# Later weight splits inside a chunk, split small projections and earlier top-k rounds in a two-layer transformer kernel on one core

## The reference

```python
h = rms_norm(x, g_norm1) * (1.0 + sc1) + sh1          # sc1, sh1 from silu(c) @ w_mod
proj = h @ w_in                                        # 17 chunks of 256 columns and three small ones
(a_u, a_v, g_q, g_k, g_v, g_r, g_a, d_q, d_k, d_v, d_iq, d_ik, d_iw, gates) = jnp.split(proj, splits, axis=-1)
y_a = gmlp_branch(gelu(a_u), gelu(a_v), ...)
log_alpha = log_sigmoid(g_a @ gla_w_gate2 + gla_b_gate) / 16          # g_a has 16 columns
y_b = rms_norm(gla_scan(g_q, g_k, g_v, log_alpha)) * silu(g_r)
score = sum over 4 heads of relu(d_iq . d_ik) * d_iw                  # d_ik has 64 columns, d_iw 4
y_c = attention of d_q over the 128 keys of the highest score, with d_q, d_k normed per head
mix = (sum of sigmoid(gates) * up projections of y_a, y_b, y_c) @ w_out
x = x + gt1 * mix; x = x + gt2 * hier_moe(norm(x))                    # 16 experts
# second layer: swiglu, then q, k, v, c_b, c_c, c_in = split(norm(h) @ w_in_2)
# forgetting attention over q, k, v; short_conv(c_c * c_in) * c_b; gates, w_out; swiglu
```

## Time and profile before

| | |
|---|---|
| median of 3 runs | 2298.84 us (2297.03 to 2301.77) |
| profiled execution | 2300.81 us |
| its span, first to last instruction | 2299.1 us |
| granted PE clock, mean | 0.945 |
| busy: PE, DVE, ACT, POOL | 94%, 43%, 31%, 27% |
| L662 (w_lo), 133 times | 618.7 us of POOL, 4653 ns each |
| L1501 (w_hi), 133 times | 254.8 us of ACT, 1916 ns each |

### The profile page before, as it was taken

The page is one execution under the profiler, slowest core; times in us unless marked ns, Lnnn a source line. Parts: engine busy times, 40 slices in busy tenths (PEclk is TensorE's granted clock), DMA queues, the critical chain, the costliest instruction groups (busy, mean ns, idle before and its releaser), DMA issues.

```text
span 2299.1 us, 28612 instructions
## 1 busy us (share of the span) xinstructions
PE 2153.3 (94%) x11806; PEld 1789.4 (78%) x11806; DVE 997.4 (43%) x1501; ACT 708.7 (31%) x880; POOL 621.3 (27%) x150
## 2 busy tenths in 40 slices
PE   7899989999998999979999998899899979999997
...
GB/s 242 31 74 56 74 74 39 174 173 195 98 55 160 341 331 332 335 56 76 90 91 91 91 91 56 55 56 48 45 92 92 89 40 92 92 91 92 100 100 37
DMA packets 176218, 261.30 MB, mean 114 GB/s; under 512 B 13209, under 2 KB 141898, under 8 KB 176126
## 3 DMA queue, kind: packets, MB, share of 16 engines
...
## 4 chain that ended last, share of the span: by engine, by line
PE 86%; DVE 7%; DMA 3%; ACT 2%; issue 1%; SPq 0%; ACTq 0%; DVEq 0%
PE PS L700 65%; PE PS L1228 6%; PE PS L1250 4%; DMA w_raw<-in_w_in 2%; DVE Hf L2072 1%; DMA m_raw<-in_w_exp_up 1%; DVE Hf L2053 1%; PE PS L856 1%; PE PS L760 1%; PE PS L1270 1%; PE PS L1194 1%; PE PS L1382 1%; ACT w_hi L1501 1%; DVE R L2084 1%; PE PS L806 1%
## 5 line engine op out<-in xcount | busy, mean ns | idle before, releaser
L662 POOL TENSOR_TENSOR w_lo<-w_raw,w_hi 128x2048 fp32r<-128x2048 f32 x133 | 618.7, 4653 | 1603.6 <-ACT w_hi L1501 1603.6
L700 PE MATMUL PS<-HH,w_hi 128*128 128x512 f32 (+1 forms) x1936 | 603.5, 350 | 43.4 <-DVE HL L2046 27.3
L700 PE MATMUL PS<-HL,w_hi 128*128 128x512 f32 (+1 forms) x1936 | 601.4, 348 | 0.0
L700 PE MATMUL PS<-HH,w_lo 128*128 128x512 f32 (+1 forms) x1936 | 598.3, 347 | 0.0
L1501 ACT ACTIVATE w_hi<-w_raw 128x2048 fp32r<-128x2048 f32 x133 | 254.8, 1916 | 821.1 <-DMA w_raw<-in_w_ffn_in 299.8
L700 PEld LDWEIGHTS PS<-HH,w_hi 128*128 128x128 f32 x1936 | 341.0, 192 | 96.2 <-issue 31.9
L700 PEld LDWEIGHTS PS<-HH,w_lo 128*128 128x128 f32 x1936 | 340.2, 192 | 45.7
L700 PEld LDWEIGHTS PS<-HL,w_hi 128*128 128x128 f32 x1936 | 340.1, 191 | 44.6
L2758 DVE TENSOR_TENSOR actf<-PS,sg 128x528 f32<-128x528 f32 (+1 forms) x44 | 30.8, 700 | 432.7 <-PE PS L700 432.7
L2769 DVE TENSOR_TENSOR yacc<-yacc,PS 128x528 f32<-128x528 f32 (+1 forms) x176 | 122.3, 695 | 106.0 <-PE PS L700 106.0
L2651 DVE TENSOR_TENSOR m_lo<-m_raw,m_hi 128x2048 fp32r<-128x2048 f32 x56 | 128.2, 2292 | 80.1 <-ACT m_hi L1814 79.4
...
## 6 DMA issues: line engine op xcount, KB each, us to landing
...
```

The source lines that it names most:

```text
L662: pool.tensor_tensor(w_lo[:, s, :], w_raw[:, s, :], w_hi[:, s, :].bitcast(F32), ALU.subtract).then_inc(split, 1)
L700: ins = mm(o, l, r, **k)
```

## The change

The small projections become one more tile of 100 columns (d_ik 64, g_a 16, 16 zero columns, d_iw 4): their weights are split by ACT and POOL into w_small_hi and w_small_lo, and PE makes their 24 L700 products between those of the first iq tile. ACT evacuates ga, ik twice, and iw_rows; PE transposes iw_rows. One small load goes.

`next_hi()` moves from ahead of a chunk's first evacuation to its middle, in the chunks gq to u and in K, Q, V, CC, CI, CB of the second layer. With gq, gk the order on ACT becomes: gq tile, relus, w_hi, gate chain, gq tile, relus. DVE does `scores(0)` before the gate's scans and `scores(4)` before `exp_arg`. Five `top_rounds` leave dsa(0) to dsa(3) (2, 2, 2, 2 become 0, 1, 1, 1) and go to the tiles of dv with the head norms (1, 1, 1, 1 become 2, 3, 2, 2).

```diff
@@ -226,3 +226,5 @@
 
-        w_small = ar("w_small", 0, [KT, 148])
+        w_small = ar("w_small", 0, [KT, 100])
+        w_small_lo = ar("w_small_lo", 0, [KT, 100], F32R)
+        w_small_hi = ar("w_small_hi", 3200, [KT, 100], F32R)
         oh_sb = ar("oh_sb", 40960, [640])
...
@@ -528,6 +533,5 @@
             w1 = wk("w_in")
-            sp.dma_start(w_small[:, :, 0:16], w1[:, :, G_A:G_A + 16]).then_inc(small_in, 16)
-            sp.dma_start(w_small[:, :, 16:80], w1[:, :, D_IK:D_IK + 64]).then_inc(small_in, 16)
-            sp.dma_start(w_small[:, :, 80:144], w1[:, :, D_IK:D_IK + 64]).then_inc(small_in, 16)
-            sp.dma_start(w_small[:, :, 144:148], w1[:, :, D_IW:D_IW + 4]).then_inc(small_in, 16)
+            sp.dma_start(w_small[:, :, 0:64], w1[:, :, D_IK:D_IK + 64]).then_inc(small_in, 16)
+            sp.dma_start(w_small[:, :, 64:80], w1[:, :, G_A:G_A + 16]).then_inc(small_in, 16)
+            sp.dma_start(w_small[:, :, 96:100], w1[:, :, D_IW:D_IW + 4]).then_inc(small_in, 16)
             sp.dma_start(w_gate2[0:16, :], a["gla_w_gate2"][0]).then_inc(small_in, 16)
@@ -648,3 +652,4 @@
             pool.memset(sel_sum[:, :], 0.0).then_inc(consts, 1)
-            pool.wait_ge(consts, 7)
+            pool.memset(w_small[:, :, 80:96], 0.0).then_inc(consts, 1)
+            pool.wait_ge(consts, 8)
             pool.memset(sel_sum[:, 3:4], 1.0).then_inc(consts, 1)
@@ -663,2 +668,4 @@
 
+            pool.wait_ge(small_hi, 1)
+            pool.tensor_tensor(w_small_lo[:, :, :], w_small[:, :, :], w_small_hi[:, :, :].bitcast(F32), ALU.subtract).then_inc(small_split, 1)
             for c in range(RING):
@@ -845,20 +852,2 @@
 
-            pe.wait_ge(small_in, 16 * 11)
-            g0, slots = W.g, []
-            ga_group, ik_group = g0, g0 + 1
-            for x in range(3):
-                slots.append(W.claim())
-                W.g += 1
-            W.g = g0
-            for k in range(KT):
-                pe.wait_ge(hh_ready, k + 1)
-                for s, c0, n in ((slots[0], 0, 16), (slots[1], 16, 128)):
-                    ins = mm(PS[0:n, s, 0, :], w_small[:, k, c0:c0 + n], Hf[:, k, 0:SEQ], start=k == 0, stop=k == KT - 1)
-                    if k == KT - 1:
-                        W.made(ins)
-                for t in range(NTOK):
-                    ins = mm(PS[:, slots[2], 0, 4 * t:4 * t + 4], Hf[:, k, P * t:P * t + P], w_small[:, k, 144:148],
-                             start=k == 0 and t == 0, stop=k == KT - 1, skip_group_check=True)
-            W.made(ins)
-            await_h(now=False)
             rh, rlo = h_operands(0, SEQ)
@@ -986,5 +975,25 @@
 
-            fm()
-            iq_group = W.g - 1
-            W.wait_released(ga_group)
+            pe.wait_ge(small_split, 1)
+            s_w = begin_chunk()
+            hi = w_hi[:, s_w, :].rearrange("p (k n) -> p k n", k=KT)
+            lo = w_lo[:, s_w, :].rearrange("p (k n) -> p k n", k=KT)
+            s_iq = W.claim()
+            W.g += 1
+            small_group = W.g
+            s_small = W.claim()
+            W.g -= 1
+            for k in range(KT):
+                pe.wait_ge(hl_ready, hcount["hl"] + k + 1)
+                iq_ins = three(outs_of(s_iq, SEQ), (hi[:, k, 0:P], lo[:, k, 0:P]), (rh(k), rlo(k)), k == 0, k == KT - 1)
+                small_ins = three([(PS[0:100, s_small, 0, :], slice(0, SEQ))], (w_small_hi[:, k, :], w_small_lo[:, k, :]),
+                                  (rh(k), rlo(k)), k == 0, k == KT - 1)
+            hcount["hl"] += KT
+            W.made(iq_ins)
+            W.made(small_ins)
+            s = W.claim()
+            for k in range(KT):
+                ins = three(outs_of(s, SEQ), (hi[:, k, P:2 * P], lo[:, k, P:2 * P]), (rh(k), rlo(k)), k == 0, k == KT - 1)
+            iq_group = W.g
+            W.made(ins)
+            W.wait_released(small_group)
             for j in range(2):
@@ -992,2 +1001,6 @@
                 W.made(mm(PS[:, s, 0, :], w_gate2[0:16, P * j:P * j + P], ga[0:16, 0:SEQ], start=True, stop=True))
+            s = W.claim()
+            for t in range(NTOK):
+                ins = nc.tensor.transpose(PS[:, s, 0, 4 * t:4 * t + 4], iw_rows[0:4, P * t:P * t + P], ident[0:4, 0:4])
+            W.made(ins)
 
...
@@ -1519,2 +1531,5 @@
                 af(squares1[:, k, :], real(k), ACT.Square).then_inc(sq_ready, 1)
+            act.wait_ge(small_in, 16 * 10)
+            act.wait_ge(consts, CONSTS)
+            af(w_small_hi[:, :, :], w_small[:, :, :], ACT.Copy).then_inc(small_hi, 1)
             root(SEQ)
@@ -1524,5 +1539,2 @@
             next_hi()
-            evac(ga[0:16, 0:SEQ], src=lambda s: PS[0:16, s, 0, :])
-            evac(ik[:, :])
-            evac(iw[:, :, :], src=lambda s: PS[:, s, 0, 0:16].rearrange("p (t h) -> p t h", h=4))
 
@@ -1586,2 +1598,7 @@
             evac(iq[:, 0, :])
+            s = W.arrive()
+            af(ga[0:16, 0:SEQ], PS[64:80, s, 0, :], ACT.Copy)
+            af(ik[0:64, :], PS[0:64, s, 0, :], ACT.Copy)
+            af(ik[64:128, :], PS[0:64, s, 0, :], ACT.Copy)
+            W.release(af(iw_rows[0:4, :], PS[96:100, s, 0, :], ACT.Copy))
             evac(iq[:, 1, :])
@@ -1589,4 +1606,9 @@
                 evac(Bc[:, j, :], ACT.Identity, bias=C1[:, V1["gla_b_gate"] + j:V1["gla_b_gate"] + j + 1])
-            W.wait_released(W.g - 2)
-            W.wait_released(W.g - 1)
+            gate_evac = W.g
+            evac(iw[:, :, :], src=lambda s: PS[:, s, 0, 0:16].rearrange("p (t h) -> p t h", h=4))
+            evac(gq[:, 0, :])
+            relus(0)
+            next_hi()
+            W.wait_released(gate_evac - 2)
+            W.wait_released(gate_evac - 1)
             for j in range(2):
@@ -1599,9 +1621,2 @@
                 af((t0, t1)[j][:, :], (t0, t1)[j][:, :], ACT.Ln, bias=eps[:, 1:2]).then_inc(gla_act, 1)
-            next_hi()
-            evac(gq[:, 0, :])
-            act.wait_ge(exp_arg, 1)
-            af(ebl[:, :, :], ebl[:, :, :], ACT.Exp, scale=1.0 / 16).then_inc(gla_act, 1)
-            relus(0)
             evac(gq[:, 1, :])
@@ -1610,9 +1625,10 @@
 
-            next_hi()
             evac(gk[:, 0, :])
             relus(8)
+            next_hi()
             evac(gk[:, 1, :])
+            act.wait_ge(exp_arg, 1)
+            af(ebl[:, :, :], ebl[:, :, :], ACT.Exp, scale=1.0 / 16).then_inc(gla_act, 1)
 
 
-            next_hi()
             for t in range(NTOK):
@@ -1620,3 +1636,4 @@
                 gla_exp(0, t)
-            next_hi()
+                if t == 1:
+                    next_hi()
             for t in range(NTOK):
@@ -1654,2 +1672,4 @@
                 gla_out(2 * t + 1)
+                if t == 0:
+                    next_hi()
 
@@ -1977,4 +1999,5 @@
             for x, c0 in enumerate(KQV):
-                next_hi()
                 for t in range(2 if x % 3 < 2 else 5):
+                    if t == (1 if x % 3 < 2 else 2):
+                        next_hi()
                     s = W.arrive()
@@ -1997,3 +2020,3 @@
             for m in range(12):
-                if m % 2 == 0:
+                if m % 2 == 1:
                     next_hi()
...
@@ -2309,4 +2331,3 @@
 
-            W.skip(4)
-            W.wait_made(W.g - 5)
+            W.skip(6)
             L.mark(v_.memset(Kp[:, :, :], 0.0))
@@ -2315,2 +2336,4 @@
             L(v_.memset(chunks(t2[:, :])[:, :, 0:1], 0.0))
+            W.skip(1)
+            scores(0)
             for j in range(2):
@@ -2322,10 +2345,7 @@
                 L.mark(v_.tensor_copy(ebl[:, j, :], chunks(Bc[:, j, :])[:, :, CHUNK - 1:CHUNK].rearrange("p c t -> p (c t)")))
+            gq_group = W.g
+            W.skip(1)
+            scores(4)
             L.wait()
             dve.sem_inc(exp_arg, 1)
-            for x in (0, 4):
-                W.skip(1)
-                scores(x)
-            gq_group = W.g - 5
             W.skip(1)
@@ -2386,3 +2406,3 @@
             W.skip(1)
-            top_rounds(1)
+            top_rounds(2)
             W.skip(1)
@@ -2392,9 +2412,9 @@
             W.skip(1)
-            top_rounds(1)
+            top_rounds(3)
             W.skip(2)
             head_columns(0)
-            top_rounds(1)
+            top_rounds(2)
             W.skip(1)
             head_columns(1)
-            top_rounds(1)
+            top_rounds(2)
 
@@ -2421,3 +2441,4 @@
                 dsa(n)
-                top_rounds(2)
+                if n > 0:
+                    top_rounds(1)
             for n in range(4, 12):
```

22 lines of the change are left out of this document (12 added, 10 removed).

## The result

| | before | after |
|---|---|---|
| median, 4 runs each | 2297.94 us (2296.87 to 2301.77) | 2265.90 us (2262.68 to 2266.08) |
| profiled execution / its span | 2300.81 / 2299.1 us | 2266.08 / 2264.3 us |

The ratio is 0.9854 [0.9837, 0.9871], 32.0 us faster. The forecast of 2266 and its range were right.

What follows compares the result with a forecast made beforehand. PE's own work was taken as 86% of the chain, so only fewer PE operations, shorter PE waits or less low-clock work help. Gains less the front's loss sum to 32.6 us: 2300.81 to 2268.2, less 2.0 gives 2266 us, range 2256 to 2284.

Steps and rivals of the forecast that it cites:

- A: Small projections, gq and gk: fp32 products replaced and PE's waits for gq and relu_s shortened; gain 8.8 us.
- front: Kernel start: POOL's making of w_small_lo may hold DVE's mod sums and move the first norm; loss of 1.5 us.
- H: Second layer: moving w_hi and POOL's split removes waits for pr and low clock, one collision kept; gain 12.0 us.
- top-k rounds: Five rounds moved from dsa(0..3) to the head norms at dv: 0 us, ends -1 and +1.
- rival 2: GLA factors: a split holds one, eats the 2.8 us cover, and PE waits 1.6 at L893; 2270 us, chance 0.05.
- B: dk chunk: w_hi no longer precedes the evacuations of dk, a wait of 1.0 us.
- C: Inverse roots: w_hi no longer precedes the evacuation of inv_rows, a wait of 1.1 us.
- D, E: First layer's v chunks: waits and low clock of 10.1 us go, DVE holds cost 3.8; gain 6.3 us.
- F, G: First layer's u chunks: shorter waits and less low clock, one hold of 2.2 left; gains 3.4 and 1.5 us.
- Rival 1: Chunks: the hold only moves, hitting a DVE step mid-chunk as at its start; 2286 us, chance 0.28 between half and whole.
- Rival 3: Chunks beside attention steps: mid-chunk splits stop PE, 4.9 us each, slower from the ninth; twelve give 2318; slower, chance 0.04.
- rival 4: Start: no head start, interleaved products wait for HL and run at low clock; A keeps 4.6; 2270 us, chance 0.05.

Runs made afterwards that it cites:

- run 4: The kernel before with only the small projections as split products, all else as before: 2297.08 us, ratio 1.0002.
- run 9: The kernel before with only the new order of the gq and gk chunks; fp32 small projections and other `next_hi()` as before: 2293.62 us, ratio 0.9985.
- run 2: The changed kernel with `next_hi()` of the first layer's chunks gv to u back at the chunk starts: 2280.72 us, ratio 0.9930.
- run 1: The changed kernel with w_hi of the second layer's chunks (K, Q, V, CC, CI, CB) back ahead of the first evacuation: 2275.80 us, ratio 0.9903.
- run 3: The changed kernel with the five top-k rounds back in the first four dsa steps: 2271.31 us, ratio 0.9882.
- run 6: The kernel before with POOL's split in two halves of 1024 columns: 2289.34 us, ratio 0.9957.
- run 5: The changed kernel with POOL's split in two halves of 1024 columns: 2265.45 us, ratio 0.9853.
- run 8: The changed kernel with w_hi of the first layer's two v chunks after the first step, not the second: 2267.26 us, ratio 0.9863.
- run 7: The changed kernel with w_hi back at the chunk's start in the second layer's last V chunk alone: 2261.88 us, ratio 0.9845.

## Why the prediction was right, and where it was not

Each part by what undoing it cost, or doing it alone gave (the letters are the prediction's):

| part | forecast | by medians | by ratios |
|---|---|---|---|
| A and front (small projections, order) | 7.3 | -0.6 (run 4) + 3.1 (run 9) | -0.5 + 3.4 |
| B to G | 13.3 | 14.8 (run 2) | 17.5 |
| H | 12.0 | 9.9 (run 1) | 11.3 |
| top-k rounds | 0 | 5.4 (run 3) | 6.4 |
| sum | 32.6 | 32.6, against 32.0 measured | 38.1, against 33.5 |

The first column of results takes the medians as they stand, from different chips; the second the differences of the ratios, times 2298. They differ by up to 2.7 for one part, and the intervals are 3 to 4 us wide to each side, so the excess of the second sum over the whole is within them; an undone move can also cost more on top of the others (dk in run 2). What stands out: A is smaller than booked, and the rounds are worth something, 2.2 in the trace of run 3, with a mechanism that can be seen there. The intervals of after and run 3 alone would leave room for nearly nothing. That the forecast came within 1 us is in part luck: A was too large by some 4, and the rounds, C and a stretch that nobody booked (below) made up for it.

- **A.** The step that was mis-sized is "Removed: 16 L856 and 32 L860 products, which hold PE from 77.3 to 88.9". That stretch was read from one execution with a low clock 2.5 us longer than in runs 6 and 9, and its end was taken as typical. The order part held: one wait of 2.4 in place of 8.1, gk's end at 132.5 (forecast 133.2). In the traces A and front give 9.5, or 7.0 without those 2.5; in time run 9, whose trace covers all of that stretch, gives 3.4 [0.7, 6.2], and with run 4 it is 2.9 by the ratios. What of the rest is chance and what is given back elsewhere stays open.
- **Front.** Right in kind and size on DVE (1.4 against 1.5), though the squares and not a mod sum were held. The cost in time is between 0 and 1.9.
- **GLA factors, rival 2.** The cover held: no wait at L882.
- **B, C.** B as forecast: 1.0 in the traces. C was booked at its wait of 1.1 and gave 2.1 (first sq_q product to first dsa logits, 46.8 before and 44.7 after; 46.8 to 47.4 in the five profiles with the old place of these `next_hi()`, 44.4 to 45.2 in the nine with the new). The rest is low clock behind that wait. Windows of before, then of after, over the same 29 products:

```profile
279.90:284.80 4.90, 4.81 (x29) 4.45 (x29) 3.01 (x6) 0.59 (x1) 2.44 (x1) 0.68 0.01 3
```
```profile
266.60:270.30 3.70, 3.68 (x29) 3.25 (x29) 3.21 (x6) 2.39 (x2) 0.58 (x1) 1.00 0.00 0
```

- **D, E.** 6.0 of 6.3 in the traces. But the working went another way than the number: the hold was put at 1.9 each and charged to PE in full. It was 4.00 and 3.67, nearly all of POOL's 4.57, and PE waited 1.85 and 1.95, so DVE had some 2 us in hand ahead of PE's need (4.00 less 0.16 for nmax unheld, less 1.85). The Trainium skill, "SBUF — State Buffer", section "Who interferes with whom", has DVE and GpSimd share one port pair under an exclusive lock; on the length of the hold the trace agrees with it, on the further loss of 2.7 per chunk that I worked out from it, not. The step of the sum that went wrong is this: a hold is not yet a wait of PE.
- **F, G.** 3.5 and 1.1 of 3.4 and 1.5. The hold in the first u chunk fell on wsT, not on the step's nmax, with the same wait (2.29 against 2.2 booked).
- **H.** The mechanism was right: undone, most of its waits come back (run 1). In a profile without low clock the gain is 11.8 (run 2's second layer), in after's 8.5. The one collision was booked at 1.6; it costs 1.2 of wait, and in three of the profiles that have it (after, runs 5 and 8) a further 3.2 to 4.8 of low clock, in two (runs 2 and 3) nothing. Run 7 takes it away: its second-layer stretch lasts 142.3 against after's 145.6, and its median is 2 to 4 lower, which its interval does not tell from none.
- **Top-k rounds.** The failed step is "of PE's waits of 1 us and more only that for pr names DVE, at neither place: 0". It looked at waits of before. After the change these steps have a hold in them, and with two rounds in each DVE has no slack left ahead of it: run 3's three steps beside the split take 4.08, 4.42 and 4.66 us, after's 3.60, 3.59 and 3.82.
- **Not foreseen.** From the first attT to the first sq_q product, before takes 31.3 us and after 29.4. Windows of before, then of after (columns as above):

```profile
218.80:250.10 31.30, 31.07 (x169) 28.31 (x168) 13.43 (x28) 5.21 (x7) 4.51 (x1) 0.67 0.09 22
```
```profile
208.30:237.70 29.40, 29.17 (x169) 26.09 (x168) 15.48 (x34) 5.38 (x7) 5.14 (x1) 0.72 0.14 32
```

The same 169 products, no wait worth the name, and a clock of 0.67 against 0.72. It is 29.4 to 29.7 in all nine profiles with the moved `next_hi()` here, and 31.2 to 31.3 in the same five with the old place (before, runs 2, 4, 6, 9). Run 2 differs from after in these calls alone, so the stretch hangs on them; by what way was not tried. The middle of the kernel, where nothing was changed (late mod product to the second layer's first attention step), gave 1.9 more in after's profile; over all fourteen profiles it runs from 1060.7 to 1066.1 us with no edit to go by, so it may be chance.

**The rivals.** Rival 1 (the hold only moves) was half right: four of PE's stalls in after stand behind a moved hold, 1.85, 1.95, 2.29 and 1.21, 7.3 in all, where the sum had booked 3.8, 2.2 and 1.6, 7.6. What it got wrong is the price. In before, ACT's w_hi, the landing and the hold stood one behind the other on PE's path; in the middle of a chunk only the hold is left, and it spends DVE's slack first. Run 6 shows that the hold was worth at least 9.6 in before; that much could be had without any move. Rival 3 would have wanted nine such stalls; there are four. Rivals 2 and 4 did not come: no wait at L882, and the full clock from 81.2.
